# Matmuls on zeros, of fixed number, in TensorE's waits of a three-block transformer kernel

## The reference, cut to what matters

```python
# first block: layer 0 even mixer, layer 1 odd mixer, each followed by a gated FFN with a 3-tap conv
h = rmsnorm(x, mix_norm_g[layer]);  x = x + even_mixer(h, ...) or odd_mixer(h, ...)
h = rmsnorm(x, ffn_norm_g[layer]);  x = x + conv_glu_ffn(h, ...)
# even mixer: z = h @ w_in (2560 columns); a 3-tap conv branch, and a branch
u = causal_dwconv(cf_a * sigmoid(cf_g), cf_conv_w) + cf_conv_b       # 31 taps, 512 channels
u = silu(layernorm(u, cf_ln_g, cf_ln_b))
# second block, for l in 0, 1
mod = silu(c) @ ada_w[l] + ada_b[l]                                   # 9 vectors of 1024
x = x + 0.5 * g1 * swiglu(modulate(rms_norm(x, ffn1_norm[l]), sh1, sc1))
z = modulate(rms_norm(x, mix_norm[l]), sh2, sc2) @ w_in[l]            # pool | cq 384 | ckv 256 | kr 64
q = rms_norm(cq, q_a_norm) @ w_q_b;  kv = rms_norm(ckv, kv_a_norm) @ w_kv_b
s = (q_nope @ k_nope + rope(q_rope) @ rope(kr)) * SOFTMAX_SCALE       # causal, 4 heads, 256 positions
x = x + g2 * (concat(y_pool, softmax(s) @ v) @ w_out)
x = x + 0.5 * g3 * swiglu(modulate(rms_norm(x, ffn2_norm[l]), sh3, sc3))
return rms_norm(x, final_norm)
```

## Time and profile before

| | |
|---|---|
| median of 3 runs | 1860.37 us (1857.49 to 1867.19) |
| profiled execution | 1858.56 us, its span 1856.8 us |
| TensorE matmuls busy | 1679.9 us, 90%, 12897 instructions |
| weight loads busy (beside the matmuls) | 1628.7 us, 88% |
| VectorE busy | 1181.7 us, 64% |
| ScalarE busy | 745.7 us, 40% |
| GpSimd busy | 11.3 us, 1% |
| read from HBM | 340.61 MB, 184 GB/s over the span |
| chain that ended last | TensorE 82%, VectorE 11%, ScalarE 3% |

### The profile page before, as it was taken

How to read it: one execution, slowest core, us unless ns; L and a number is a source line. 1 busy time by engine, 2 the same in 40 slices (tenths; PEclk the granted TensorE clock), 3 DMA queues, 4 the chain that set the end, 5 groups by cost and what they waited for, 6 DMA issues and landing times.

```text
span 1856.8 us, 30132 instructions
## 1 busy us (share of the span) xinstructions
PE 1679.9 (90%) x12897; PEld 1628.7 (88%) x12897; DVE 1181.7 (64%) x1279; ACT 745.7 (40%) x752; POOL 11.3 (1%) x25
## 2 busy tenths in 40 slices
PE   4927999988889999999989679999999987799998
PEld 3926999987778999999989579999999987589998
DVE  5795788765957887577763646776554464464444
ACT  3404544434444444433333334343433343344333
POOL 2000000000000000000000000000000000000000
PEclk7968999979999999899988789999899998799999
DMA  6422788734326886488862326886355543235551
GB/s 194 136 91 68 260 307 306 257 106 127 117 69 219 308 301 231 132 309 306 296 218 90 101 68 230 304 308 216 116 185 181 181 131 116 68 117 185 181 193 49
DMA packets 230498, 342.61 MB, mean 185 GB/s; under 512 B 6971, under 2 KB 193825, under 8 KB 230433
## 3 DMA queue, kind: packets, MB, share of 16 engines
q1 hardware_dynamic: 228608, 339.50, 54.6%
q10 hardware_dynamic: 1152, 1.40, 0.2%
q0 software_dynamic: 672, 0.79, 0.2%
HBM read 340.61 MB, written 1.05 MB: 184 GB/s over the span
## 4 chain that ended last, share of the span: by engine, by line
PE 82%; DVE 11%; ACT 3%; issue 2%; DMA 1%; ACTq 1%; DVEq 0%; SPq 0%
PE PS L526 73%; PE PS L544 3%; DVE Z L1391 3%; PE PS L554 2%; DVE wl L1141 2%; PE PS L624 2%; ACT wh L833 1%; DVE RS L1490 1%; DVE T L1164 1%; DVE RS L1159 1%; ACTq L822 1%; PE PS L646 1%; PE PS L635 1%; DMA raw<-ffn_w_down 0%; DVE RS L1579 0%
## 5 line engine op out<-in xcount | busy, mean ns | idle before, releaser
L526 PE MATMUL PS<-HH,wh 128*128 128x256 f32 x2884 | 836.8, 291 | 61.8 <-DVE HL L1587 24.8
L1141 DVE TENSOR_TENSOR wl<-raw,wh 128x2048 fp32r<-128x2048 f32 (+2 forms) x257 | 573.0, 2232 | 454.2 <-ACT wh L833 453.6
L526 PE MATMUL PS<-HH,wl 128*128 128x256 f32 x2884 | 828.8, 288 | 0.0
L526 PE MATMUL PS<-HL,wh 128*128 128x256 f32 x2884 | 809.8, 287 | 0.0
L833 ACT ACTIVATE wh<-raw 128x2048 fp32r<-128x2048 f32 (+2 forms) x257 | 478.3, 1863 | 440.3 <-PE PS L526 420.7
L526 PEld LDWEIGHTS PS<-HH,wh 128*128 128x128 f32 x2884 | 566.9, 197 | 71.2 <-issue 62.5
L526 PEld LDWEIGHTS PS<-HH,wl 128*128 128x128 f32 x2884 | 567.0, 197 | 0.2
L526 PEld LDWEIGHTS PS<-HL,wh 128*128 128x128 f32 x2884 | 556.3, 196 | 1.4 <-issue 1.2
L526 PE MATMUL PS<-FH,wh 128*128 128x256 f32 x1056 | 298.5, 283 | 15.5 <-DVE FL L1262 15.5
L526 PE MATMUL PS<-FL,wh 128*128 128x256 f32 x1056 | 297.0, 281 | 0.0
L526 PE MATMUL PS<-FH,wl 128*128 128x256 f32 x1056 | 296.9, 281 | 0.0
(11 more groups left out here) (205 smaller groups left out, 962.3 us busy)
## 6 DMA issues: line engine op xcount, KB each, us to landing
ada<-ada_w SPq DMA_DIRECT2D x144, 512.0 KB, 5.8
raw<-ffn_w_gate SPq DMA_DIRECT2D x66, 1024.0 KB, 5.4
raw<-ffn_w_up SPq DMA_DIRECT2D x66, 1024.0 KB, 5.4
raw<-ffn_w_down SPq DMA_DIRECT2D x66, 1024.0 KB, 5.0
raw<-od_w_in SPq DMA_DIRECT2D x13, 1024.0 KB, 5.2
raw<-ev_w_in SPq DMA_DIRECT2D x10, 1024.0 KB, 6.0
raw<-w_in SPq DMA_DIRECT2D x8, 1024.0 KB, 5.4
raw<-w_out SPq DMA_DIRECT2D x8, 1024.0 KB, 5.0
```

What stands on the lines that cost most here:

```text
L526: last = mm(dst, lhsT=lhs(a, k), rhs=rhs(b, k), start=first and i == 0, stop=first and i == len(order) - 1, skip_group_check=not first)
L1141: last = tt(dst(wl), src, dst(wh).bitcast(F32), ALU.subtract)
```

## The change

A helper `spin(n, bk)` issues n matmuls of zeros (ZB, bf16, 128 x 128 stationary, 512 columns moving) into one bank whose contents nobody needs. TensorE's program calls it behind the statistic of the norms that have no `ada_units` and aren't the last (mix0, ffn0, ffn1, fb0, fb1: 12; w1: 16), between the last ev_in projection and the layer norm's first sum (112, behind a wait that bank 5 was read), behind each of that norm's two sums (12 and 20), behind the projections of w_in ahead of the products with w_q_b (48), and around scores, transposes and values of the second block's attention (8, 6, 14, 3, 4, 4; all but the first into bank 6). The wait for V's copies moves ahead of the first of these. The other engines' programs and all transfers are the same.

```diff
--- before.py
+++ after.py
@@ -527,6 +527,11 @@
                               stop=first and i == len(order) - 1, skip_group_check=not first)
                 return last
 
+            def spin(n, bk=5):
+
+                for _ in range(n):
+                    mm(pairs(bank(bk), P), lhsT=ZB[:], rhs=over(ZB[:], 4), start=True, stop=True)
+
             def weights(n, k_tiles, off=0):
 
                 pe.wait_ge(split_done, n + 1 + 6 * off)
@@ -556,6 +561,8 @@
                 last.then_inc(stat, 1)
                 if name in ADA_GAP:
                     ada_units(name)
+                elif name != "final":
+                    spin(16 if name == "w1" else 12)
 
             def project(n, bk, k_tiles=KD, fill=None, token=False, narrow=P):
 
@@ -665,19 +672,24 @@
             pe.wait_ge(ev("zeros"), 1)
 
 
-            norm("mix0")
             for u in range(10):
+                if u == 0:
+                    norm("mix0")
                 if u >= 6:
                     pe.wait_ge(z_out, u - 5)
                 project(U0["ev_in"] + u, u % 6, fill="mix0" if u == 0 else None)
+            pe.wait_ge(z_out, 6)
+            spin(112)
             pe.wait_ge(ev("cf_conv"), 4)
             for t in range(4):
                 last = mm(bank(7, 0, S), lhsT=cn("ones"), rhs=cols(Z, 1144, 4)[:, t, :], start=t == 0, stop=t == 3)
             last.then_inc(ev("ln_sum"), 1)
+            spin(12)
             pe.wait_ge(ev("ln_sq"), 1)
             for t in range(4):
                 last = mm(bank(7, 0, S), lhsT=cn("ones"), rhs=cols(WK, 0, 4)[:, t, :], start=t == 0, stop=t == 3)
             last.then_inc(ev("ln_var"), 1)
+            spin(20)
             for u in range(4):
                 project(U0["ev_out"] + u, u, fill="y_ev" if u == 0 else None)
             norm("ffn0")
@@ -741,6 +753,7 @@
                                 last = mm(bank(7, c, S), lhsT=cn("ones"), rhs=cols(WK, 0, 5)[:, a + t, :],
                                           start=t == 0, stop=t == k - 1)
                         last.then_inc(ev("mq_stat"), 1)
+                spin(48)
 
                 for i in range(2):
                     w = weights(U0[f"q_b{l}"] + i, 3)
@@ -778,16 +791,22 @@
                 last.then_inc(ev("pool_full"), 1)
                 rounds = latent_rounds()
                 scores, turn, values = attend("mla", l, rounds)
+                pe.wait_ge(ev("v_out"), 2 * l + 2)
+                spin(8)
                 pe.wait_ge(ev("rope"), l + 1)
-                pe.wait_ge(ev("v_out"), 2 * l + 2)
                 pe.wait_ge(ev("kn_out"), l + 1)
                 scores(0)
+                spin(6, 6)
                 pe.wait_ge(ev("y_pool"), 4 * l + 4)
                 scores(1)
+                spin(14, 6)
                 turn(0)
+                spin(3, 6)
                 values(0)
                 turn(1)
+                spin(4, 6)
                 values(1)
+                spin(4, 6)
                 for u in range(4):
                     project(U0[f"w_out{l}"] + u, u, fill=f"yw{l}" if u == 0 else None)
                 norm(f"fb{l}")
```

## The result

The changed kernel took 1830.03 us (median of 4 runs, 1829.49 to 1834.74), the kernel before 1859.63 us (4 runs): ratio 0.9839, 95% interval [0.9807, 0.9871]. The forecast was 1833 us, the range 1821 to 1848. The profiled execution is 28.6 us shorter (span 1828.2 against 1856.8).

The account below looks back on a forecast made before the run. TensorE bounds FFNs and projections, and dense matmuls behind waits run at 1.2 GHz. Terms 10.0 + 3.2 + 3.1 + 14.6 = 30.9 us, less an eighth, 27 us; 1860.4 - 27 = 1833 us, range 1821 to 1848.

Parts of the forecast that it names:

- Term 1: Six norms: zeros fit the waits, so dense products behind the last piece of HH run at 2.4 GHz; 10.0 us.
- HH's short bursts: Behind norms, only short bursts of matmuls until HH is complete, so the clock will sometimes be lost after all.
- Term 2: Query norm, both layers: 48 zeros in the 12.40 us wait keep the products behind at full clock; 3.2 us.
- Term 4: Second block's attention: scores, values and turn(1) at full clock; 7.3 us a layer, 14.6 us in both.
- The step of the six zeros on the path: Attention, between scores(0) and scores(1): six zeros end 0.7 us behind the pooled output that scores(1) waits for.
- Rival (a): Clock held for the products but not through attention: 1844 to 1854 us, say 1847; chance 0.14.
- Term 3: Beside the long convolution and in its layer norm: variance 1.6 us, dense work behind 1.5 us; together 3.1 us.
- The variance's 8 matmuls then take half: Layer norm's variance sum at full clock: 1.8 us for 3.42 us, a gain of 1.6 us.
- The 12 behind it [...] bring the clock back: 12 zeros after the layer norm's first sum fit the 5.32 us ahead of the variance and restore the clock.
- The eighth taken off: Summed gain cut from 30.9 to 27 us because nearly full waits will sometimes lose the clock after all.
- Rival (b): Saved time absorbed: transfers set the end of ffn0, ffn1 and fb0, about 10 us lost, 1843 us; chance 0.12.
- Rival (c): Zeros don't count as activity: the clock falls during the fills, 38 us slower, 1898 us; chance 0.05.

Follow-up runs that it names:

- e6_norms_28: The changed kernel with 28 zeros in each of the six norms instead of 12 or 16: 1833.84 us, against 1836.91 for the changed kernel.
- e9_more_ada: Changed kernel plus zeros in dilated attention, ahead of ffn0's and fa0's last down units, in the final norm and among four norms' modulation column sums: 1843.09 us.
- e10_longer: Changed kernel plus zeros in dilated attention, last down units and final norm; 20 per norm, 54 before the query product, no 112: 1826.31 us against 1835.23.

## Why the prediction was right, and where it was off

**The mechanism and the sum.** Reading the price of the clock from the dense stretches alone, not from 275 us at 1.2 GHz, was right: that total fell by more than half (a clock of 0.967 over 1828.2 us leaves 121 us), and the gain is 28.6 us, where half of the difference would have been 77. Wide matmuls of zeros did it where thin ones in the same places didn't; the order of the waits had no part, and ones did as well as zeros.

**Term 1**: 10.5 for 10.0 where the clock held in all six norms. What the prediction said of the other executions ("will sometimes lose the clock after all") is shown by the norms-only profile, 4.5 us with three of six lost, and by both repeats. I said HH's short bursts are the cause; the windows agree in place, no run removed the bursts. In e6_norms_28, where the zeros reach over the first of them, the clock held behind all six.

**Term 2**: 3.1 for 3.2. **Term 4**: 14.0 for 14.6, and 13.4 alone. The step of the six zeros on the path was 1.1 us (pooled output at 1049.75, scores(1) at 1050.87) for the 0.7 estimated. Rival (a), attention unheld, is refuted: PEclk 1.00 over 9.79 us.

The Trainium skill, TensorE: Matmul & The Clock Gate, Part 1, puts the ramp penalty at under 1% of a typical kernel span; an estimate by that page, taken as a cap on the gain, is 18.6 us. It says so of the slow matmuls of one ramp; to make it a cap on all the ramps behind this kernel's waits was my reading. The stages outside attention sum to 15.8 us, within it; with attention 29.8 us were won, 1.6% of the span, and the repeats gained 21.0 and 23.6 us, so for the whole kernel the measurement decides against such a cap.

**Term 3** is the term that was mis-sized: 2.2 for 3.1. "The variance's 8 matmuls then take half" did not hold: 2.58 us instead of 1.8, because the clock was lost again at 139.6, in the middle of the variance's sum, with 2.79 us idle between the 12 zeros and it; that this wait is the cause is argued, not tested. "The 12 behind it [...] bring the clock back" did not hold either: it was back before the first of them. The 112 do nothing for the time, as predicted and as the run without them shows.

**The eighth taken off** gave the right total of the profiled execution for a wrong reason, by luck. I attributed it to the filled waits; there all nine held, and 3.8 us were lost in the dilated attention instead, while 2.4 came in fa0, neither of which has zeros or was in the sum. In the two repeats the reason holds: filled waits did lose the clock, in four places and in three. Over the three measurements the mean of the medians, 1834.1 us, is 1 us over the forecast; but the kernel before came out 1.6 us under the 1860.4 that I subtracted from, and the mean gain is 24.7 us for 27.

**Rival (b)**, absorption, is refuted by the stages: 2.2 us reach the end of ffn1 and of fb0. **Rival (c)** is refuted by the clock over the fills.

## What to carry to other kernels

A wait of TensorE can cost twice: once as a wait, and again as slow matmuls behind it; the second part is read from the dense stretches at PEclk 0.50 that follow waits, not from the mean clock. Filling a wait with wide matmuls on zeros mostly wins that part back if the fill ends near the wait's end, and an overhang was cheap where the operands behind came piece by piece. The one fill that ended 6.4 us early was worth nothing, and neither were thin ones; zeros that no wait covers only cost, however high they raise the mean clock (e9_more_ada). And since places with and without a fill may win or lose the clock from one execution to the next, judge such a change by several of them.

## What was not expected of the hardware

The clock fell under 224 gapless matmuls of 16 columns with their weight loads (PEclk 0.77 in a window with 3.00 of 3.00 us busy). In code that no change touched, the dilated attention, the low stretch was 10.24 us in one profile and 20.47 us in another, 32.4 or 36.1 us for the stage, and the changed kernel itself showed both; so it isn't the zeros elsewhere that decide. The stage fa0, untouched as well, took 213.5 us in one profile of the changed kernel and 215.3 in another. And in e10_longer, layer 0, the clock fell 2.7 us into round 0's scores, in the midst of work and with eight wide zeros ahead of it. What decides in a given execution was not isolated.
